# Recurrent mixer of a two-block model: gates without reciprocals, roots in pieces, half of the output projection fed chunk by chunk

## What is computed

```python
def rg_lru(x, w_a, b_a, w_x, b_x, lam):
    xb = x.reshape(bsz, s, N_LRU_BLOCKS, LRU_BLOCK)
    r = sigmoid(einsum("bsnd,nde->bsne", xb, w_a).reshape(bsz, s, w) + b_a)
    i = sigmoid(einsum("bsnd,nde->bsne", xb, w_x).reshape(bsz, s, w) + b_x)
    log_a = (-LRU_C * r) * softplus(-lam)
    a = exp(log_a)
    mult = sqrt(-expm1(2.0 * log_a))
    u = mult * (i * x)
    # h[t] = a[t] * h[t-1] + u[t]

def recurrent_mixer(hn, ...):
    gate, xr = split(hn @ w_in, 2)
    xr = causal_depthwise_conv(xr, conv_w, conv_b)
    y = rg_lru(xr, ...)
    return (y * gelu(gate)) @ w_out
```

## Time and profile before

| | us |
|---|---|
| median of 3 runs | 2021.09 |
| lowest, highest | 2018.03, 2022.53 |
| profiled execution, own time | 2019.94 |
| its span, first to last instruction | 2018.1 |
| PE busy | 1816.4 (90%) |
| DVE busy | 1369.9 (68%) |
| ACT busy | 799.4 (40%) |

### The profile page before, as it was taken

One profiled execution on the slowest core, in us unless ns is written; L12 is line 12 of the kernel. 1 busy time (PEld: TensorE's weight loads), 2 busy tenths in 40 slices (PEclk: granted clock), 3 DMA queues, 4 the chain that ended last, 5 costly groups with the idle time before them and its releaser, 6 DMA issues. The chain is left out here.

```text
span 2018.1 us, 28781 instructions
## 1 busy us (share of the span) xinstructions
PE 1816.4 (90%) x11914; PEld 1623.7 (80%) x11914; DVE 1369.9 (68%) x1856; ACT 799.4 (40%) x1138; POOL 153.7 (8%) x156
## 2 busy tenths in 40 slices
PE   5788989899999999779899998955899999898999
PEld 1578668678788878676789998954899999788999
DVE  2596565889966775664567666889787876755544
ACT  1321454343213431334455455352443434445452
POOL 0123100011000110141001010001000001100000
PEclk9778679899999999787999999986899999889999
DMA  6342100334364445330034644623687885313552
GB/s 246 142 167 87 60 1 22 146 145 162 141 233 186 181 162 194 128 142 25 10 131 149 205 145 161 251 102 122 236 328 296 327 323 186 109 53 136 189 185 86
DMA packets 46658, 317.87 MB, mean 158 GB/s; under 512 B 5248, under 2 KB 6272, under 8 KB 12608
## 3 DMA queue, kind: packets, MB, share of 16 engines
q1 hardware_dynamic: 45936, 312.22, 42.2%
q0 software_dynamic: 592, 3.81, 0.5%
HBM read 314.96 MB, written 1.05 MB: 157 GB/s over the span
## 5 line engine op out<-in xcount | busy, mean ns | idle before, releaser
L1375 PE MATMUL PM<-Hhi,whi 128*128 128x256 f32 (+1 forms) x1766 | 567.3, 321 | 72.3 <-DVE Hlo L1247 31.0
L1376 PE MATMUL PM<-Hlo,whi 128*128 128x256 f32 (+1 forms) x1766 | 554.8, 314 | 0.0
L1377 PE MATMUL PM<-Hhi,wlo 128*128 128x256 f32 (+1 forms) x1766 | 554.8, 314 | 0.0
L873 DVE TENSOR_TENSOR wlo<-raw,whi 128x2048 fp32r<-128x2048 f32 (+3 forms) x205 | 443.0, 2161 | 139.2 <-ACT whi L621 138.9
L621 ACT ACTIVATE whi<-raw 128x2048 fp32r<-128x2048 f32 (+3 forms) x205 | 365.2, 1781 | 187.0 <-PE PM L1377 159.1
L1375 PEld LDWEIGHTS PM<-Hhi,whi 128*128 128x128 f32 x1766 | 344.8, 195 | 102.0 <-issue 53.6
L1376 PEld LDWEIGHTS PM<-Hlo,whi 128*128 128x128 f32 x1766 | 346.4, 196 | 17.0 <-issue 0.2
L1377 PEld LDWEIGHTS PM<-Hhi,wlo 128*128 128x128 f32 x1766 | 345.6, 196 | 17.6
L902 DVE SCALAR_TENSOR_TENSOR acc<-raw,silc,acc 128x512 f32<-128x512 f32 x384 | 286.1, 807 | 1.6 <-DVE wlo L873 0.2
L1375 PE MATMUL PM<-Ghi,whi 128*128 128x256 f32 (+1 forms) x864 | 270.8, 313 | 11.7 <-DVE Glo L1099 11.7
L1376 PE MATMUL PM<-Glo,whi 128*128 128x256 f32 (+1 forms) x864 | 265.7, 308 | 0.0
(11 more groups left out here) (186 smaller groups left out, 1998.2 us busy)
## 6 DMA issues: line engine op xcount, KB each, us to landing
raw<-in_ada SPq DMA_DIRECT2D x104, 1024.0 KB, 4.8
raw<-in_wm SPq DMA_DIRECT2D x91, 1024.0 KB, 4.9
raw<-in_wl SPq DMA_DIRECT2D x68, 1024.0 KB, 4.9
raw<-in_wl SPq DMA_DIRECT2D x32, 704.0 KB, 4.4
raw<-in_wm SPq DMA_DIRECT2D x8, 704.0 KB, 4.1
raw<-in_wm SPq DMA_DIRECT2D x4, 768.0 KB, 4.9
X<-in_x SPq DMA_DIRECT2D x1, 2048.0 KB, 9.4
bias<-in_bias POOLq DMA_DIRECT2D x1, 2048.0 KB, 11.2
```

The lines of the kernel that those rows point to most:

```text
L873: dve.tensor_tensor(wslot(wlo, i, usize(u)), slot_raw(n, usize(u)), wslot(whi, i, usize(u)).bitcast(F32), ALU.subtract)\
L1375: pe.matmul(out, st_hi, mv_hi, start=first, stop=False)
L1376: pe.matmul(out, st_hi, mv_lo, start=False, stop=False)
L1377: return pe.matmul(out, st_lo, mv_hi, start=False, stop=last)
```

## The change

- `evac` of the gates on ACT: the two sigmoids become tanh of half the argument, and after the tanh into `LA` there is an exp per chunk, in place in `rs`. The four factors come from four small operations in the prologue. sigmoid(z) = (1 + tanh(z/2))/2, and 1 - exp(-2v) = tanh(v) * (1 + exp(-2v)), so DVE needs no reciprocal. A maximum with 1e-30 per unit takes the place of the clamp over all of `XR`; the factors 1/2 are made up for in the root's scale (-0.25).
- The root and the multiply with it go in four pieces (`LSTEPS`), each root waiting only for its gate units.
- Chunks 0 to 2 of `XR` are split in the step of the last lin unit, ahead of its own evacuation.
- lout 0 to 3 become three units "lpart" (4, 4 and 3 input chunks by 512 outputs), which accumulate four output chunks side by side in one half of `PM`, each input chunk as the scan delivers it. The third one's weights are split inside the scan step; its residual adds four chunks. Units are 204 now; lout 4 to 7 are 120 to 123.
- The squares have four slots of 256 columns instead of two where the width is 256.
- `ada_plan`: the pieces that stood at units 100, 102, ... 110 stand at 99, 101, ... 109; those at 117 to 121 (lout 0 to 4) stand at 119 to 123 (lpart 2, lout 4 to 7).

```diff
...
 GATE_UNITS = [list(range(a, min(a + 2, NL))) for a in range(0, NL, 2)]
+LPARTS = [[0, 1, 2, 3], [4, 5, 6, 7], [8, 9, 10]]
+LSTEPS = [[0, 1], [2, 3, 4, 5], [6, 7, 8, 9], [10]]
...
         add("lin", "M0", n, KD, 256, 256)
     for n in range(len(GATE_UNITS)):
         add("lgate", "M0", n, 2 * sum(len(GATES[j]) for j in GATE_UNITS[n]), 128, 256)
-    for n in range(KD):
+    for n, ks in enumerate(LPARTS):
+        add("lpart", "M0", n, len(ks), 512, 256)
+    for n in range(4, KD):
         add("lout", "M0", n, NL, 128, 256)
...
-                if key == ("lout", 0):
+                if key == ("lpart", 0):
                     prog.append(("lscan",))
...
+    if u["kind"] == "lpart" and u["idx"] < len(LPARTS) - 1:
+        return None
...
+    if u["kind"] == "lpart":
+        return [0, 1, 2, 3]
...
-    for a, b, by in ((1, 7, 1), (8, 10, 1), (12, 50, 1), (52, 56, 1), (100, 111, 2), (117, 122, 1), (125, 163, 1)):
+    for a, b, by in ((1, 7, 1), (8, 10, 1), (12, 50, 1), (52, 56, 1), (99, 110, 2), (119, 124, 1), (124, 162, 1)):
...
-                    if k >= 2:
-                        act.wait_ge(*at("sumsq", (n, k - 2)))
-                    act.activation(tslot(2 + k % 2, W), X[:, k * 512:k * 512 + W], ACT.Square).then_inc(*tick("sq", (n, k)))
+                    d = 1024 // W
+                    if k >= d:
+                        act.wait_ge(*at("sumsq", (n, k - d)))
+                    act.activation(sqslot(k, W), X[:, k * 512:k * 512 + W], ACT.Square).then_inc(*tick("sq", (n, k)))
...
+                    if j == NL - 1:
+                        for c in range(3):
+                            split_x(c)
...
                     rs = tslot(u["idx"] % 2)
+                    act.wait_ge(*at("prep", "gates"))
...
                     for c, j in enumerate(js):
-                        act.activation(rs[:, c * 256:c * 256 + 256], pm(i, c * 512, 256), ACT.Sigmoid, bias=fcol("lba", j))\
+                        act.activation(rs[:, c * 256:c * 256 + 256], pm(i, c * 512, 256), ACT.Tanh, scale=0.5, bias=lcol(8, j))\
                             .then_inc(*C.link("act_chain"))
                     for c, j in enumerate(js):
-                        ins = act.activation(LU[:, j * 256:j * 256 + 256], pm(i, c * 512 + 256, 256), ACT.Sigmoid, bias=fcol("lbx", j))
+                        ins = act.activation(LU[:, j * 256:j * 256 + 256], pm(i, c * 512 + 256, 256), ACT.Tanh, scale=0.5, bias=lcol(9, j))
...
                     for c, j in enumerate(js):
 
-                        ins = act.activation(LA[:, j * 256:j * 256 + 256], rs[:, c * 256:c * 256 + 256], ACT.Tanh,
-                                             scale=lk[:, 5 * NL + j:5 * NL + j + 1])
+                        ins = act.activation(LA[:, j * 256:j * 256 + 256], rs[:, c * 256:c * 256 + 256], ACT.Tanh, scale=lcol(6, j), bias=lcol(6, j))
+                    ins.then_inc(*C.link("act_chain"))
+                    act.wait_ge(*C.last)
+                    for c, j in enumerate(js):
+                        ins = act.activation(rs[:, c * 256:c * 256 + 256], rs[:, c * 256:c * 256 + 256], ACT.Exp, scale=lcol(7, j), bias=lcol(7, j))
                     ins.then_inc(*tick("lr", u["idx"]))
...
                 elif step[0] == "lscan":
-                    act.wait_ge(*at("lm", 0))
-                    for h in range(2):
-                        q = slice(h * 6 * 256, min((h + 1) * 6, NL) * 256)
-                        act.activation(XR[:, q], XR[:, q], ACT.Sqrt, scale=-1.0).then_inc(*tick("ls", h))
+                    for p, js in enumerate(LSTEPS):
+                        q = slice(js[0] * 256, (js[-1] + 1) * 256)
+                        act.wait_ge(*at("la", js[-1] // 2))
+                        act.activation(XR[:, q], XR[:, q], ACT.Sqrt, scale=-0.25).then_inc(*tick("ls", p))
                     for j in range(NL):
                         act.wait_ge(*at("ly", j))
                         act.activation(Hhi[:, j * 256:j * 256 + 256], LU[:, j * 256:j * 256 + 256], ACT.Copy).then_inc(*tick("hhi", ("y", j)))
+                        if j == 2:
+                            split_hi(first_of("lpart", "M0") + 2)
...
+                    if (u["kind"], u["idx"]) != ("lpart", 0):
+                        split_hi(i + 2)
...
+            link(dve.tensor_scalar(lk[:, 6 * NL:7 * NL], res, 0.5, None, ALU.mult))
+            link(dve.tensor_scalar(lk[:, 7 * NL:8 * NL], res, -1.0, None, ALU.mult))
+            link(dve.tensor_scalar(lk[:, 8 * NL:9 * NL], feat[:, FEAT["lba"]:FEAT["lba"] + NL], 0.5, None, ALU.mult))
+            dve.tensor_scalar(lk[:, 9 * NL:10 * NL], feat[:, FEAT["lbx"]:FEAT["lbx"] + NL], 0.5, None, ALU.mult).then_inc(*tick("prep", "gates"))
...
+                        ins = dve.scalar_tensor_tensor(out=dst, in0=pm(i, m * each + who * 256, 256), scalar=modc(v, who, c),
...
+                elif kind in ("out", "down", "lout", "w2") or (kind, u["idx"]) == ("lpart", len(LPARTS) - 1):
...
+                    if j == NL - 1:
+                        for c in range(3):
+                            split_x(c)
...
-                    s = tslot(2 + u["idx"] % 2, w)
+                    s, ap = tslot(2 + u["idx"] % 2, w), tslot(u["idx"] % 2, w)
                     th, u_, x_ = (b[:, js[0] * 256:js[0] * 256 + w] for b in (LA, LU, XR))
 
-                    link(dve.tensor_scalar(s, th, 1.0, None, ALU.add))
-                    link(dve.reciprocal(s, s))
-                    link(dve.scalar_tensor_tensor(out=s, in0=s, scalar=2.0, in1=th, op0=ALU.mult, op1=ALU.mult))
+                    link(dve.scalar_tensor_tensor(out=s, in0=ap, scalar=1.0, in1=th, op0=ALU.add, op1=ALU.mult))
+                    link(dve.tensor_scalar(s, s, 1e-30, None, ALU.max))
                     dve.tensor_scalar(th, s, -1.0, 1.0, ALU.mult, ALU.add).then_inc(*C.link("dve_chain"))
-                    link(dve.tensor_tensor(u_, u_, x_, ALU.mult))
+                    link(dve.scalar_tensor_tensor(out=u_, in0=u_, scalar=1.0, in1=x_, op0=ALU.add, op1=ALU.mult))
                     dve.scalar_tensor_tensor(out=x_, in0=s, scalar=2.0, in1=s, op0=ALU.subtract, op1=ALU.mult).then_inc(*tick("la", u["idx"]))
...
                 elif step[0] == "lscan":
-                    dve.wait_ge(*at("la", len(GATE_UNITS) - 1))
-
-                    dve.tensor_scalar(XR[:, :], XR[:, :], -1e-30, None, ALU.min).then_inc(*tick("lm", 0))
-                    for h in range(2):
-                        q = slice(h * 6 * 256, min((h + 1) * 6, NL) * 256)
-                        dve.wait_ge(*at("ls", h))
+                    for p, js in enumerate(LSTEPS):
+                        q = slice(js[0] * 256, (js[-1] + 1) * 256)
+                        dve.wait_ge(*at("ls", p))
                         link(dve.tensor_tensor(LU[:, q], LU[:, q], XR[:, q], ALU.mult))
-                        for j in range(h * 6, min((h + 1) * 6, NL)):
+                        for j in js:
                             q = slice(j * 256, j * 256 + 256)
                             dve.tensor_tensor_scan(XR[:, q], LA[:, q], LU[:, q], 0.0, ALU.mult, ALU.add).then_inc(*tick("lh", j))
                             if j >= 2:
                                 scan_lo(j - 2)
+                            if j == 5:
+                                split_lo(first_of("lpart", "M0") + 2)
...
+                if kind == "lpart" or (kind == "lout" and UNITS[i - 1]["kind"] == "lpart"):
+                    pe.wait_ge(*at("pm_act", first_of("lpart", "M0") - 1))
...
+                elif kind == "lpart":
+                    for m, k in enumerate(LPARTS[u["idx"]]):
+                        pe.wait_ge(*at("hlo", ("y", k)))
+                        for c in range(4):
+                            w0 = m * 512 + c * 128
+                            ins = three(pm(first_of("lpart", "M0"), c * 256, 256), wslot(whi, i, 128, w0), wslot(wlo, i, 128, w0),
+                                        mh[:, k * 256:k * 256 + 256], ml[:, k * 256:k * 256 + 256], k == 0 and c % 2 == 0, k == NL - 1 and c % 2 == 1)
...
+    wl = f["lru_w_out_2"][0]
+    for ks in LPARTS:
+        seq += _units_of(wl[ks[0] * P:(ks[-1] + 1) * P], len(ks), [ar(512)])
+    seq += _units_of(wl, NL, group(D, 128)[4:])
...
```

More of the change, by code:

```diff
@@ L216, in ada_plan @@
     assert -8 <= left <= 0, left
-    for i in range(162, 162 + left, -1):
+    for i in range(161, 161 + left, -1):
         n[i] = 0
@@ L642, in _, with split_x @@
             squares(0, range(KD), 512)
+            def split_x(j):
+                act.wait_ge(*at("lxd", j))
+                act.activation(Hhi[:, j * 256:j * 256 + 256], XR[:, j * 256:j * 256 + 256], ACT.Copy).then_inc(*tick("hhi", ("x", j)))
             def ffn_stage2(u):
@@ L834, in _ @@
                 elif step[0] == "lsplit":
-                    act.wait_ge(*at("unit", first_of("lgate", "M0") - 1))
-                    for j in range(NL):
-                        act.wait_ge(*at("lxd", j))
```

(17 more changed lines are left out.)

31 lines of the change are left out of this document (16 added, 15 removed).

## The result

| | before | changed |
|---|---|---|
| median, us (4 runs each, side by side) | 2021.81 | 1988.85 |
| lowest, highest | 2018.03, 2023.91 | 1985.31, 1990.39 |
| profiled execution, own time | 2019.94 | 1990.39 |
| its span | 2018.1 | 1988.6 |

The ratio is 0.9837, with a 95% interval of 0.9817 to 0.9856. The prediction was 1987.0 in a range of 1982 to 1998. It had 34.1 us saved; the medians say 33.0 and the two profiled executions 29.5.

A forecast was written before the change was run, and what follows sets the result against it. DVE's chain was taken to bound the recurrent mixer, PE the rest. The gain accumulated to 34.75 us at the last residual, less 0.65 at norm 5: 2021.1 - 34.1 = 1987.0 us, range 1982 to 1998.

The forecast's parts named there:

- What bounds the kernel: Recurrent mixer: DVE's chain through gates, scan and projection is the bound; outside the mixer PE is.
- Term 1: Start of the gates: DVE gets the first gate unit at 1324.65 instead of 1329.0 us, gain 4.4 us.
- Term 2: Six gate units: bound passes from DVE to ACT, 4.8 us a unit; gain 21.5 us including the earlier start.
- Term 3: Roots and scan: no clamp or root wait; last chunk split at 1372.0 instead of 1394.66, gain so far 22.7 us.
- Term 4: Output projection: chunk-wise feed regains full clock, DVE ends late by 2 us; last residual at 1397.6, gain 34.75 us.
- Term 5: Norm 5: last residual to reciprocal takes 2.95 us instead of 2.28, loss 0.65 us.
- Covered, at nothing: Prologue operations, modulation piece ahead of norm 4, squares' slots, load queue: no cost; the piece would cost 2 us uncovered.
- (a): Rival, output projection: PE's clock does not come back in the chunk-wise feed, 8 us later, 1995 us; chance 0.10.
- (c): Rival: low clock holds through the projection's remaining units into the MLP, slower than before, 2042 us; chance 0.02.
- (b): Rival, gates: tanh and exp each reload their table in every unit, 12.8 us, 2000 us; chance 0.04.
- (d): Rival: DVE's order is looser than summed, 3 to 6 us more gained, 1982 us or below; chance 0.05.
- The sum: Whole kernel: 34.75 - 0.65 = 34.1 us saved, median from 2021.1 to 1987.0 us.

The follow-up runs named there:

- e12: Changed kernel with the scale of the gates' second tanh and exp a constant 0.01 instead of a column; 1986.67 us, ratio 0.9819.
- e4: Changed kernel with the old gate start: conv chunks split together behind lin 10, modulation piece one unit later; 1994.92 us, ratio 0.9867.
- e2: Kernel before with the new gate arithmetic and the root in four pieces without the clamp, everything else old; 2002.41 us, ratio 0.9907.
- e11: The changed kernel itself, nothing altered, timed and profiled once more; 1988.82 us, ratio 0.9834.

## Why the prediction was right, step by step

**What bounds the kernel** held: DVE's chain of gates, scan and projection set the end of the mixer; the parts are worth 17.9, 6.7 and 6.5 us in sequence, and what follows keeps the gain. (For the MLP the rows have 424 matmuls in 50 us, not 421; the spacing is 0.12 either way.)

**Term 1** (4.4 expected) measured 88.6 - 84.5 = 4.1. The exp started 1.29 us behind the start of the table load, so the term was not 1.4 us smaller.

**Term 2** is the term that was mis-sized. The bound passed to ACT, as said, but a unit took 5.24 us and not 2.42 + 0.95 + 1.47 = 4.84. The prediction priced the second tanh as before (0.82 for two) and the exp at 0.95; with a scale and a bias column each, and a wait between them, they take 1.13 and 1.00 from start to start. e12 shows the column to be the main part: 0.37 us less per unit without it, where the miss was 0.40. The Trainium skill, "ScalarE: Activation LUTs", section "What ACT_TABLE_LOAD costs", gives about 93 ns for each such column operand, and the runs agree (0.91 and 1.09 for two activations). The row of a tanh with one column could not show what two would cost. Terms 1 and 2 gave 19.4 of 21.5.

**Term 3** held as a sum: 112.0 to 133.6 is 21.6 us, as from 109.9 to 131.5. There was no wait for the root. But two misses cancel, which is luck. From start to start the three multiplies behind the first scan took 1.72, 1.24 and 0.99 us (predicted 1.6, 1.4 and 0.45; by the prediction's own two rates the second is 1.2) and the weight split 2.21 (predicted 1.8), together 0.9 too little. The scans and splits of chunks took 14.7 us where 15.75 was carried over from before.

**Term 4** was 1.0 short: 26.6 us from the last split to the last residual for 25.6. ACT's split came 1.06 and 1.14 us late instead of 0.9 and 0.5; the second of these waited for its load. DVE, not PE, was late, as said: PE ended 3.2 us ahead of the last residual. What the step missed is that a second limit of nearly the same length lay under it, the ring of 5.15 us, so that the pieces were not worth their 2.65 us each. The old trace had it already: the last three residuals start at 1422.05, 1427.19 and 1432.35, with DVE idle for ACT's split in between.

```profile
1427.19 0.48 DVE L1025 SCALAR_TENSOR_TENSOR X<-PM,mod,X 128x256 f32<-128x256 f32 x1
1430.02 2.29 DVE L873 TENSOR_TENSOR wlo<-raw,whi 128x2048 fp32r<-128x2048 f32 x1 [2.34 <-ACT whi L621]
```

**Term 5**: 2.81 us from last residual to reciprocal, 2.95 predicted.

**Covered, at nothing** held for the piece ahead of norm 4: 2.80 us from residual to reciprocal with it (changed kernel) and without it (before, e4).

**The rivals.** (a) the clock staying low in the feed, (c) low into the MLP and (b) a load in every unit did not happen. For (a), e2 and the changed kernel show the difference between a thin and a dense feed: 0.50 through the scan, against full spacing after 4.4 us. (d), more than summed, did not happen either.

**The sum**: 34.1 predicted, 31.1 in the mixer by the profiles. By the table of marks 0.4 us are missed up to the first gate unit, 1.7 in the gates, nothing in the scan and 1.0 in the projection. The medians say 33.0, with an interval from 29 to 37, so the profile's number is inside. The same kernel profiled again (e11) has a span 33.1 us below before: 30.8 from norm 4 to norm 5, 2.9 behind it, less 0.6 ahead of norm 4. So the mixer repeats, and some 2 us come and go outside it; before's own profile is 1.9 us under its median too. That the median came nearer to the forecast (1988.85 for 1987.0) than the mixer did is therefore partly luck. Where these 2 us lie in the other runs of before stays open, as there is one profile of it.

## What to carry to other kernels

Before pricing a small job by the engine that does most of it, follow its results: these modulation pieces cost nothing on DVE where DVE has room, but a pair cost 1.9 us on PE where PE was the bound. When two queues wait for each other through different steps of neighbouring units, add the loop up once; no work saved outside the loop goes below it, and it may already show in the old trace. And when a bound is to pass from one engine to another, price each new instruction in the exact form it will have, since that engine's old rows were never on the path.
